# Two units on unscaled tokens behind the first two norms, and four modulation units as row products on VectorE

## What is computed

```python
def rmsnorm(x, g):
    y = xf * lax.rsqrt(jnp.mean(xf * xf, axis=-1, keepdims=True) + EPS)
    return (y * g.astype(jnp.float32)).astype(x.dtype)
...
        h = rmsnorm(x, norm1_g[l])
        (hg_q, hg_f, ...) = jnp.split(h @ w_in[l], split_at, axis=-1)
...
        x = x + mixed @ w_out[l]
        u = causal_dwconv(rmsnorm(x, norm2_g[l]) @ w_up[l], ffn_conv_w[l], ffn_conv_b[l])
...
def modulation(cond, w_ada, b_ada):
    m = jax.nn.silu(cond) @ w_ada + b_ada
```

## Time and profile before

| | |
|---|---|
| median of 3 runs | 1656.17 us (1655.36 to 1656.5) |
| the profiled execution, its own time | 1660.86 us |
| its span, first to last instruction | 1659.0 us |
| TensorE busy | 1602.6 us, 97% |
| VectorE busy | 1236.9 us, 75% |
| ScalarE busy | 881.1 us, 53% |
| mean granted TensorE clock | 0.991 |

### The profile page before, as it was taken

How to read it: one execution, slowest core, us unless ns; L and a number is a source line. 1 busy time by engine, 2 the same in 40 slices (tenths; PEclk the granted TensorE clock), 3 DMA queues, 4 the chain that set the end, 5 groups by cost and what they waited for, 6 DMA issues and landing times.

```text
span 1659.0 us, 34573 instructions
## 1 busy us (share of the span) xinstructions
PE 1602.6 (97%) x14802; PEld 1454.3 (88%) x14802; DVE 1236.9 (75%) x2091; ACT 881.1 (53%) x1344; POOL 135.4 (8%) x98
## 2 busy tenths in 40 slices
PE   8999999999999999999988999999999998899999
PEld 7999888898999999998867888888877897799999
DVE  5575489587777886588866788877888788678864
ACT  4535645538546675456775544323433456666653
POOL 0003540000000110100000011110110000001100
PEclk9999999999999999999999999999999999999999
DMA  7655555454455554521102243464345222045544
GB/s 279 245 218 227 193 209 186 175 208 173 153 178 183 201 194 158 185 106 65 65 2 94 89 149 136 160 225 152 127 162 181 109 102 103 28 153 191 191 164 142
DMA packets 41129, 259.67 MB, mean 157 GB/s; under 512 B 4368, under 2 KB 7696, under 8 KB 14480
## 3 DMA queue, kind: packets, MB, share of 16 engines
q1 hardware_dynamic: 40976, 257.46, 43.4%
HBM read 256.39 MB, written 1.05 MB: 155 GB/s over the span
## 4 chain that ended last, share of the span: by engine, by line
PE 69%; DVE 22%; ACT 5%; DMA 2%; issue 2%; DVEq 0%; SPq 0%; ACTq 0%
PE acc_psum L209 21%; PE acc_psum L210 20%; PE acc_psum L211 20%; DVE w_low_sb L174 5%; DVE mod_products L336 3%; DVE u_filtered L2117 2%; DVE ring_sb L336 2%; PE acc_psum L218 2%; DMA ring_sb<-in_w_up 1%; ACT w_high_sb L162 1%; PE acc_psum L2610 1%; PE acc_psum L272 1%; ACT norm_rt_sb L2870 1%; PE acc_psum L2639 1%; DVE h_low_sb L502 1%
## 5 line engine op out<-in xcount | busy, mean ns | idle before, releaser
L209 PE MATMUL acc_psum<-h_high_sb,w_high_sb 128*128 128x256 f32 (+1 forms) x2176 | 657.2, 302 | 4.5 <-DVE h_low_sb L502 1.9
L210 PE MATMUL acc_psum<-h_low_sb,w_high_sb 128*128 128x256 f32 (+1 forms) x2176 | 649.6, 299 | 0.0
L211 PE MATMUL acc_psum<-h_high_sb,w_low_sb 128*128 128x256 f32 (+1 forms) x2176 | 649.6, 299 | 0.0
L162 ACT ACTIVATE w_high_sb<-ring_sb 128x1024 fp32r<-128x1024 f32 (+2 forms) x412 | 387.0, 989 | 364.7 <-PE acc_psum L211 219.2
L174 DVE TENSOR_TENSOR w_low_sb<-ring_sb,w_high_sb 128x1024 fp32r<-128x1024 f32 (+2 forms) x384 | 421.6, 1140 | 123.9 <-ACT w_high_sb L162 114.0
L209 PEld LDWEIGHTS acc_psum<-h_high_sb,w_high_sb 128*128 128x128 f32 x2176 | 412.7, 190 | 31.5 <-issue 12.6
L210 PEld LDWEIGHTS acc_psum<-h_low_sb,w_high_sb 128*128 128x128 f32 x2176 | 410.6, 189 | 15.5 <-issue 0.5
L211 PEld LDWEIGHTS acc_psum<-h_high_sb,w_low_sb 128*128 128x128 f32 x2176 | 410.7, 189 | 15.0
L2117 DVE SCALAR_TENSOR_TENSOR u_filtered<-acc_psum,par_sb,u_filtered 128x255 f32<-128x255 f32 (+2 forms) x264 | 150.7, 571 | 47.3 <-ACT u_filtered L2258 28.3
L209 PE MATMUL acc_psum<-u_high,w_high_sb 128*128 128x256 f32 (+1 forms) x539 | 169.7, 315 | 4.4 <-DVE w_low_sb L174 2.8
L209 PE MATMUL acc_psum<-w_high_sb,h_high_sb 128*128 128x256 f32 x560 | 165.9, 296 | 2.9 <-DVE h_low_sb L502 2.3
(11 more groups left out here) (310 smaller groups left out, 1831.2 us busy)
## 6 DMA issues: line engine op xcount, KB each, us to landing
ring_sb<-in_w_in SPq DMA_DIRECT2D x68, 1024.0 KB, 6.8
ring_sb<-in_w_up SPq DMA_DIRECT2D x66, 1024.0 KB, 4.9
ring_sb<-in_w_down SPq DMA_DIRECT2D x48, 704.0 KB, 4.2
ring_sb<-in_w_ada SPq DMA_DIRECT2D x24, 1024.0 KB, 4.8
ring_sb<-in_w_ada_rows SPq DMA_DIRECT2D x24, 1024.0 KB, 4.9
ring_sb<-in_w_out SPq DMA_DIRECT2D x12, 1024.0 KB, 4.8
ring_sb<-in_w_br_hg SPq DMA_DIRECT2D x4, 1024.0 KB, 6.8
ring_sb<-in_w_br_ml SPq DMA_DIRECT2D x4, 1024.0 KB, 5.0
```

Source lines behind the costliest of these rows:

```text
L162: self.nc.scalar.activation(self.high[:, self.shifted(c, g, piece)], self.ring[:, c % RING, piece], ACT.Copy)\
L209: nc.tensor.matmul(out, sh, mh, start=start, stop=False)
L210: nc.tensor.matmul(out, sh, ml, start=False, stop=False)
L211: return nc.tensor.matmul(out, sl, mh, start=False, stop=stop)
```

## The change

Four things. (1) Units 0 and 1 of the hybrid block take x times gain, not divided by the token's root, as operand; VectorE multiplies their results by the row, kept in SBUF. The norm's sums are made behind the fourth tile of unit 0, the row is spread in unit 1, and the scaled operand is wanted from unit 2. The fills of both norms, except the 20 at the start, are gone. The gain of the first norm is loaded by itself, weight unit 1 ahead of the other parameters. (2) The same behind the second norm, for the first two units of the feed forward; sums and row stand in its unit 0. (3) 20 units of the first layer's modulation stay column rides, behind units 11, 13, ..., 49, in two groups of 10. (4) The first 4 units of the row store are now the last 4 of the first layer; their slots follow units 3, 5, 7 and 9, and their dots stand in VectorE's list at n = 2, 4, 6 and 8, behind the split of unit n + 1. For that the condition rows are loaded at the start as well, ahead of the ring's later slots.

```diff
-RIDES = tuple(range(1, 2 * (N_ADA * P // UNIT), 2))
+RIDES = tuple(range(11, 51, 2))
+EARLY_ROWS = 4
+EARLY_RIDES = (3, 5, 7, 9)
...
-    TOGETHER = 12
+    TOGETHER = 10
...
     def dot(self, dve, n, c, tiles=(0, 1)):
...
+        if 0 in tiles:
+            core.wait_loaded(dve, c)
+            if n in self.begun:
+
+                dve.wait_ge(self.rows_ready.handle, self.begun.index(n) + 1)
+            if n:
+
+                dve.wait_ge(self.multiplied.handle, n)
         for s in range(2):
-            for j in range(2):
-                t, row = 2 * n + j, slot[:, j, :]
+            for j in tiles:
+                row, (bias, result) = slot[:, j, :], self.result(n, j)
...
+    def unscaled_high(self, act, t):
+
+        self.core.nc.scalar.activation(self.unscaled(t)[0], self.X[:, t, 0:S], ACT.Copy, scale=self.streams[0].gain(t))\
+            .then_inc(*self.highed[0].one())
+
+    def unscaled_low(self, dve, t):
+
+        dve.wait_ge(*self.at(self.highed[0], t + 1))
+        high, low = self.unscaled(t)
+        dve.scalar_tensor_tensor(low, self.X[:, t, 0:S], self.streams[0].gain(t), high.bitcast(F32), ALU.mult, ALU.subtract)\
+            .then_inc(*self.lowed[0].one())
+
+    def keep_row(self, act):
+
+        act.wait_ge(*self.at(self.spread_out, 1))
+        self.core.nc.scalar.activation(self.row, self.spread_row(0), ACT.Copy).then_inc(*self.kept.one())
...
             def _(sp):
+                g_ = PAR_AT["norm1"][1]
                 for half in range(2):
...
+                    if half == 0:
+                        sp.dma_start(par[:, 0:g_], a["par"][:, 0:g_]).then_inc(*sig("first_gain_ready").dma())
...
                 core.load(sp, 0)
-                sp.dma_start(par[:, :], a["par"]).then_inc(*par_ready.dma())
+                core.load(sp, 1)
+                sp.dma_start(par[:, g_:], a["par"][:, g_:]).then_inc(*par_ready.dma())
...
             sp.dma_start(flat(wg), a["w_gates"]).then_inc(*wg_ready.dma())
-            core.release(sp, UNITS, mod)
+            rows.fetch(sp, a["cond_rows"])
+            core.release(sp, UNITS, (mod, rows))
```

TensorE, hybrid block:

```diff
                     else:
                         mm = product(nc, ps, [p[:, kk, j * P:(j + 1) * P] for p in w],
+                                     norm1.unscaled(kk) if n < norm1.raw else [p[:, kk, 0:S] for p in x],
...
+                    if n == 0 and (kk, j) == (3, 1):
+                        norm1.folded_sums(pe, folded)
+                    if n == 1 and a_ == 1:
+
+                        pe.wait_ge(identity.handle, 16)
+                        norm1.spread(pe)
...
             keep_busy(core, psum[:, 6, :], 20)
-            norm1.folded_sums(pe, folded)
-
-            pe.wait_ge(identity.handle, 16)
-            norm1.spread(pe)
...
-                if n > START["out"]:
-                    norm2.sums(pe, n - 1 - START["out"])
-            norm2.sums(pe, DT // 2 - 1)
-            norm2.spread(pe)
```

ScalarE, hybrid block (loop over n, in this order):

```diff
+            for half in range(2):
+
+                act.wait_ge(x_ready[half].handle, 16)
+                norm1.square(act, 2 * half)
+                norm1.square(act, 2 * half + 1)
+                if half == 0:
+
+                    act.wait_ge(sig("first_gain_ready").handle, 16)
+                else:
+                    core.split_high(act, 0)
+                for t in range(4 * half, 4 * half + 4):
+                    norm1.unscaled_high(act, t)
 
             for n in range(UNITS + 1):
                 if n < UNITS:
                     high(n + 1)
                 if n == 0:
+                    norm1.root(act, core.eps[:, 0:1])
...
+                if n == 1:
+                    norm1.keep_row(act)
+                if n == 2:
+                    for t in range(DT // 2, DT):
+                        norm1.high(act, t)
                 if n >= 1:
                     evict(n - 1)
+                if n == 1:
+                    for t in range(DT // 2):
+                        norm1.high(act, t)
...
+                if n == 2:
+                    rows.activate(act)
-                if n == 5:
+                if n == 4:
                     gate_weights_high(act)
```

VectorE, hybrid block:

```diff
+                if n < norm1.raw:
+
+                    dve.wait_ge(*done.at(n + 1))
+                    nc.vector.tensor_tensor(q[:, 2 * u:2 * u + 2, :], psum[:, n % BANKS, :].rearrange("p (a b) -> p a b", a=2),
+                                            norm1.row.unsqueeze(1).broadcast_to([P, 2, S]), ALU.mult).then_inc(*norm1.scaled.one())
...
                 if n < UNITS:
                     low(n + 1)
+                if n == 0:
+                    norm1.reciprocal(dve)
+                if n == 1:
+
+                    dve.wait_ge(*norm1.at(norm1.kept, 1))
+                if 1 <= n <= norm1.raw:
+                    evict(n - 1)
+                if n == 1:
+                    norm1.parts(dve)
                 for i in steps[1:]:
                     hg_step(dve, i)
+                if n + 1 in EARLY_RIDES:
+                    rows.dot(dve, EARLY_RIDES.index(n + 1), core.place(n + 1) + 1)
...
-                if n == 4:
+                if n == 3:
                     nc.vector.memset(flat(attn), 0.0).then_inc(*mk_kept.one())
...
+                if n > START["out"]:
+                    for t in (2 * (n - 1 - START["out"]), 2 * (n - 1 - START["out"]) + 1):
+                        norm2.unscaled_low(dve, t)
```

The feed forward's up stage, where `raw` is 2 behind the second norm and 0 elsewhere (TensorE, VectorE, ScalarE):

```diff
+                    if raw and n == 0 and (k, j) == (3, 1):
+                        norm.sums(pe, DT // 2 - 1)
+                    if raw and n == 0 and (k, j) == (6, 1):
+                        norm.spread(pe)
...
+            elif raw:
+                core.split_low(dve, g0 + 1, "dve")
+
+                dve.wait_ge(*norm.at(norm.kept, 1))
+                scale(0)
+                core.split_low(dve, g0 + 2, "dve")
+                norm.parts(dve)
+                core.split_low(dve, g0 + 3, "dve")
+                for i in range(1, 2 * raw):
+                    scale(i)
...
                 first_weights()
+                if raw:
+                    norm.keep_row(act)
+
+                    act.wait_ge(*acc.at(2))
+                    core.split_high(act, g0 + 2)
                 if norm:
                     norm.highs(act)
+                if raw:
+
+                    act.wait_ge(*acc.at(4))
+                    core.split_high(act, g0 + 3)
```

More of the change, by code:

```diff
@@ L1549, in _ @@
         def _(sp):
[L1550 removed]
+            for c in range(2, RING):
                 core.load(sp, c)
@@ L2149, in up @@
     split = isinstance(norm, TwoNorms)
+    raw = norm.raw if norm and not split else 0
     def bank(i):
@@ L2399, in _ @@
                     core.split_low(dve, g0 + n + 1, "dve")
+                for j in range(2) if both else ():
+                    if n + 1 - j in rides:
+                        side.dot(dve, m0 + rides.index(n + 1 - j), core.place(g0 + n + 1 - j) + 1, (j,))
                 if h == per - 1:
```

206 lines of the change are left out of this document (125 added, 81 removed).

## The result

| | before | changed |
|---|---|---|
| median, first set | 1655.76 us (4 runs) | 1667.65 us (1664.42 to 1670.17, 4 runs) |
| median, second set | 1657.68 us (27 runs) | 1665.33 us (1659.68 to 1674.77, 10 runs) |
| ratio, first set | | 1.0062, 95% interval 1.0039 to 1.0085 |
| ratio, second set | | 1.0053, 1.0032 to 1.0074 |
| the profiled execution | 1660.86 us, span 1659.0 | 1667.72 us, span 1665.9 |

The changed kernel is slower by 0.5 to 0.6%, 8 to 12 us. The forecast was 1654.0, its range 1646 to 1659.

The account below looks back on a forecast made before the run. TensorE bounds the kernel (69% of the chain that ended last), with VectorE's list deciding where it is later. Terms: -0.5 at unit 10, +1.2 for unit 49's ride, -2.8 second norm: -2.1 us, 1654.0 on the median, range 1646 to 1659.

Parts of the forecast that it names:

- part 3: VectorE's list in units 2 to 10: waits eat 8.3 of 8.8 us, leaving -0.5 us at unit 10; moved reduction costs nothing.
- Part 4: Second norm: feed forward's unit 4 begins at 534.1 instead of 536.9, 2.8 us gained and kept.
- part 1: Start: first product at 11.8 instead of 16.93, 5.1 us gained, less 0.7 inside the stream and 1.6 for lower clock.
- the wait of unit 2: In the middle of unit 2, TensorE waits 1.0 us for the scaled norm's last highs and low.
- part 2: Column rides cost 1.20 us each: units 1, 3, 5, 7, 9 lose theirs (6.0 us), unit 49 gets one (1.2).
- The two later dots: Units 7 to 10: 10.1 us of VectorE against 11.1 of TensorE, so these dots hide.
- The charge for the clock behind that wait: After the 4.6 us wait ahead of unit 4: lower clock, half of it under VectorE's list, 0.7 us charged.
- (a): Units 2 to 10: the dots hide and the 8.3 us of waits go; 1645.7, or half, 1650; chance 0.22.
- (b): Both early stretches: the clock stays high, 1.6 + 0.7 us more gained, 1651.7; chance 0.12.
- (c): VectorE's list in units 2 to 10: longer dots make it slower, 1659.6 or 1666; chance 0.10.
- (d): Second norm gives nothing, its values move behind unit 2 and VectorE is as late as before; 1656.8; chance 0.04.
- (e): Start: the small gain load's latency, 1.9 us, stands in series ahead of x and weights; 1655.9; chance 0.03.

Follow-up runs that it names:

- e13: Changed kernel padded by 128 and 16 bytes a partition so later tiles keep the addresses of the kernel before; 1661.61 us, 1.0009.
- e18: Changed kernel at the addresses of the kernel before, with the second norm as before; 1659.67 us, 1.0001.
- e2: Changed kernel with the second norm as before, addresses not padded back; 1666.25 us, 1.0046.
- e14: Kernel before with later tiles shifted 16 bytes a partition higher, no instruction changed; 1661.76 us, 1.0021.
- e3: Changed kernel without early dots, all 24 first-layer modulation units as column rides from unit 3; 1655.10 us, 0.9976.
- e9: Changed kernel with TensorE's two long waits filled with products of ones, 19 and 20; 1666.62 us, 1.0057.
- e4: Changed kernel with early row slots behind units 5, 7, 9, 10, each dot two places later in VectorE's list; 1669.24 us, 1.0062.
- e10: Changed kernel with the four row slots moved behind down half units 2, 5, 8, 11 of the feed forward; 1675.02 us, 1.0095.
- e15: Changed kernel at the addresses of before, with the four early dots moved into the first attention layer; 1681.29 us, 1.0126.
- e1: Changed kernel with the feed forward's filter lag taken back by two iterations that issue no split; 1666.34 us, 1.0041.
- e7: Changed kernel with the feed forward's filter lag taken back in four half-unit steps; 1664.81 us, 1.0044.
- e8: Changed kernel with the column rides of e3 and the four half-unit catch-up steps of e7; 1656.62 us, 0.9991.
- e12: Changed kernel with the down-stage dots of e10 and the four half-unit catch-up steps of e7; 1667.18 us, 1.0054.
- e17: e3 with the second norm as before, at the addresses of the kernel before; 1654.80 us, 0.9973.

## Why the prediction was wrong

**The step that failed most** stands in part 3: "The reduction moves from units 25 and 49 to 31 and 51, same four products: nothing". What was counted there were instructions. The same edit makes two tiles 144 bytes shorter, all tiles behind them move, and that costs 7 to 9 us of the 8 to 12, give or take 5 (e13 against the changed kernel; e18 against e2 gives 0.45% again). e14 shows the effect alone in the kernel before, with another shift and 3.5 us. At equal addresses the change is at 1.0009, 1.5 us above the kernel before and not 2.1 below it, which the interval (0.9990 to 1.0027) doesn't tell apart. None of the rivals was of this kind: all of them sought the loss in waits.

**Part 4, "so it stays gained", failed too.** The 2.8 us at the feed forward's unit 4 were there: 534.09 for 534.1, and 537.03 before. But VectorE's free time of a stage was read as free anywhere in it. The kernel's order puts the filters two units further back and leaves them there; at the end of the stage the debt falls due at once, 4.59 us of wait for 0.76 before, then the lower clock. In the traces that takes back more than was gained, some 2.5 us net by unit 94; in the times undoing the part gives 0.1 to 0.3% in the table, with an uncertainty of 0.25%.

**What held:** the start (part 1: 11.8 for 11.72, the lower clock once; the wait of unit 2; over the seventeen traces with this start the first product comes at 11.40 to 13.84, the median 12.00), part 2's ride price (unit 7 takes 5.44 us in the changed kernel and 6.53 with a ride in e3: 1.1 for 1.20), and part 3's list: a wait of 4.6 that the trace shows as 4.52, released by the split behind the dot. The two later dots hid, as forecast: TensorE has no idle time from 42.80 to 220. Unit 10 begins at 80.93 for 80.62 before, +0.3 us where -0.5 stood. Why the first dot is late, in two rows of ScalarE and VectorE of the changed kernel:

```profile
34.55 1.90 ACT L344 ACTIVATE arena_hybrid<-arena_hybrid 128x2048 f32<-128x2048 f32 x1
```
```profile
36.60 1.28 DVE L365 CUSTOM_DVE_ANT_0 norm_rt_sb<-ring_sb,arena_hybrid,par_sb 128x1024 f32<-128x1024 f32 x1 [2.62 <-ACT arena_hybrid L344]
```

The charge for the clock behind that wait held too. From 42.10 to 48.90 the lower clock cost TensorE some 3.0 us, half of 6.10 busy, but the prediction charged only what sticks out beyond VectorE's list, 0.7; that was 13.86 less 13.35 (e9), 0.5. Unit 6 came at 56.66 for 56.2, since the list was 0.4 us longer than written. The charge in part 1 was right in this trace: 1.6 charged, half of 3.08 measured.

**The rivals.** (a): no, the first dot did not hide, the wait was there, and e4, e10, e15 looked for room for the four in three places and found none. Keeping only the two later dots, which hid, was not tried. (b): no, the clock fell at both places in both traces of the changed kernel; but of the seventeen traces with this start six (e1, e3, e7, e8, e12, e17) have the full clock on the first products, so the charge of 1.6 is right for some executions only. (c) named the right sign for a wrong reason: dots lasted 1.28 us a product, the list was as long as written. (d): no, the gain came, and went later. (e): unit 0's split began at 9.28 (before 9.38), so in this trace the small load had no latency in series. Over the seventeen traces with the small load it began at 8.96 to 11.40, the median 9.56, and over the three without at 9.11 to 9.38: some 0.3 us, and in two traces (e9, e10) 1.2 us or more; whether those two come from the small load is not known. The 2 us of fixed cost that the Trainium skill, DMA: Bandwidth & Descriptors, gives in "Anatomy of one DMA", for GpSimd's path, while SP issues the loads here, did not add to the start in the others.

## What to carry to other kernels

Before costing an edit at nothing, look at what it allocates: a tile that changes its size moves the operands of every later matmul, and a run that pads the tile back costs two lines and separates that from all else. Before calling a lower clock a loss, look at what the products behind it would wait for at full clock. A lag between two engines that a stage doesn't work off is a debt that falls due at its end, and idle tenths of an engine over a stage don't show that it has room for a task of 5 us at a given place. Where gapless stretches can differ by 4% from one execution to the next, compare traces stage by stage and judge the whole by ten runs or more.

## What was not expected of the hardware

- **Several spacings of the same products.** 0.1134 or 0.1178 us for 256 columns (in e14, behind 1600 us, also a mix of 0.115 to 0.123); for 512 columns 0.2267, or wider, in the first down stage 0.229 and 0.238 in turn in the changed kernel and 0.230 to 0.235 in e14. It can stay for long (1040 products at 0.1134 from 520.80 in the kernel before). In some stretches it falls anew in each execution, in others it follows the operands' addresses: wide in the attention layer's two down stages in ten traces of ten with moved tiles, in none of ten with the tiles where they were. The Trainium skill, SBUF — State Buffer, section "Operand start alignment", lets an fp32 operand start at any multiple of 4 bytes and says that this is about legality, not speed; here 16 bytes decided over 243 or 238 products in 55 us. Which operand and which multiple matter was not tried; 144 bytes down and 16 up leave the same remainder in steps of 32 bytes, which two shifts are too few to settle.
- **Executions spread by 17 us.** 30 runs of the kernel before lay between 1649.58 and 1666.72, while its first three lay within 1.2. Four runs of the changed kernel could not have shown what 0.3% needs.
